# A two-layer MoE step on one core: the router moves into the output projection, its table is made on chip, the first expert and the extra tiles stay unsplit, and VectorE takes every low half of the experts' weights

## The reference, cut to what matters

```python
h = h + g1 * (merged @ w_out)                        # output projection, 1024x1024
u2 = rmsnorm(h, norm2_g) * (1.0 + sc2) + sh2         # sc2, sh2: one pair for latent, one for context
scores = softmax(u2 @ w_router)                      # 1024x16, 16 experts in 4 groups
# best group by its two best (scores + bias), then its two best experts; weights renormalised
y = sum over the token's 2 experts of  w * ((silu(u2 @ w_gate[e]) * (u2 @ w_up[e])) @ w_down[e])
h = h + g2 * y                                       # w_gate, w_up 1024x256; w_down 256x1024
```

## Time and profile before

| | |
|---|---|
| median of three runs | 2220.95 us |
| the profiled execution's own time | 2221.34 us |
| its span, first to last instruction | 2219.8 us (1.5 us lie around it) |
| busy share: TensorE, VectorE, ScalarE, POOL | 74%, 62%, 37%, 32% |
| mean granted clock of TensorE | 0.852 of 2.4 GHz |
| DMA: moved, mean rate | 303.96 MB, 137 GB/s |

### The profile page before, as it was taken

The page is one execution under the profiler, slowest core; times in us unless marked ns, Lnnn a source line. Parts: engine busy times, 40 slices in busy tenths (PEclk is TensorE's granted clock), DMA queues, the critical chain, the costliest instruction groups (busy, mean ns, idle before and its releaser), DMA issues.

```text
span 2219.8 us, 27630 instructions
## 1 busy us (share of the span) xinstructions
PE 1646.8 (74%) x8896; PEld 1399.6 (63%) x8896; DVE 1377.6 (62%) x2021; ACT 815.4 (37%) x1260; POOL 708.7 (32%) x303
## 2 busy tenths in 40 slices
PE   3799678778996941999338968777899886449970
PEld 1579455578996741777237955556899875437760
DVE  1457677889936362676362947778996356427744
ACT  3112555651123040666132225556212322126641
POOL 4222000024323133697133310000433232348951
PEclk6799789998998955999669978999999997569985
DMA  8221144312213431798621203441132162229956
GB/s 310 64 59 57 62 135 153 105 29 66 78 49 104 180 149 54 263 361 331 236 77 57 76 25 133 142 144 48 39 86 58 45 240 104 105 81 356 369 194 251
DMA packets 130409, 303.96 MB, mean 137 GB/s; under 512 B 11593, under 2 KB 81353, under 8 KB 109953
## 3 DMA queue, kind: packets, MB, share of 16 engines
q1 hardware_dynamic: 104096, 224.41, 29.5%
q10 hardware_dynamic: 10560, 40.90, 4.8%
q0 software_dynamic: 15600, 36.78, 4.7%
HBM read 279.76 MB, written 39.58 MB: 144 GB/s over the span
## 4 chain that ended last, share of the span: by engine, by line
PE 39%; DVE 21%; issue 18%; DMA 10%; POOL 6%; ACT 5%; DVEq 1%; ACTq 0%; POOLq 0%; SPq 0%
PE ps L484 10%; PE ps L470 5%; PE ps L662 5%; POOL w_lo L1941 4%; PE ps L548 4%; PE ps L720 3%; DMA raw<-in_w_down 3%; PE ps L416 2%; DVE probs L1455 2%; PE ps L528 2%; DVE gu_lo L1284 2%; PE ps L692 1%; PE ps L557 1%; PE ps L530 1%; DMA raw<-in_w_gate 1%
## 5 line engine op out<-in xcount | busy, mean ns | idle before, releaser
L1941 POOL TENSOR_TENSOR w_lo<-raw,w_hi 128x2048 fp32r<-128x2048 f32 (+1 forms) x68 | 299.8, 4414 | 738.6 <-ACT w_hi L944 704.6
L484 PE MATMUL ps<-u_hi,w_hi 128*128 128x320 f32 x768 | 245.2, 319 | 39.9 <-POOL w_lo L1941 30.1
L484 PE MATMUL ps<-u_lo,w_hi 128*128 128x320 f32 x768 | 243.4, 317 | 0.0
L484 PE MATMUL ps<-u_hi,w_lo 128*128 128x320 f32 x768 | 242.9, 316 | 0.0
L944 ACT ACTIVATE w_hi<-raw 128x2048 fp32r<-128x2048 f32 (+1 forms) x68 | 109.2, 1609 | 360.5 <-PE ps L470 155.4
L1566 DVE SCALAR_TENSOR_TENSOR cv<-glu,convw,cv 128x670 f32<-128x670 f32 x240 | 234.7, 1053 | 0.0
L484 PEld LDWEIGHTS ps<-u_hi,w_hi 128*128 128x128 f32 x768 | 149.6, 195 | 43.6 <-issue 33.3
L1471 DVE TENSOR_TENSOR pt_lo<-ps,pt_hi 128x512 fp32r<-128x512 f32 x160 | 108.6, 690 | 66.6 <-ACT pt_hi L1051 64.4
L484 PEld LDWEIGHTS ps<-u_hi,w_lo 128*128 128x128 f32 x768 | 149.6, 195 | 0.0
L484 PEld LDWEIGHTS ps<-u_lo,w_hi 128*128 128x128 f32 x768 | 149.5, 195 | 0.1
L720 PE MATMUL ps<-gu_hi,xt_hi 128*128 128x512 f32 x272 | 115.0, 423 | 37.6 <-DVE xt_lo L1770 27.1
(11 more groups left out here) (335 smaller groups left out, 4263.5 us busy)
## 6 DMA issues: line engine op xcount, KB each, us to landing
raw<-in_w_ada SPq DMA_DIRECT2D x52, 1024.0 KB, 8.8
raw<-in_w_in SPq DMA_DIRECT2D x48, 512.0 KB
raw_x<-in_w_gate SPq DMA_DIRECT2D x20, 1024.0 KB, 5.2
raw_x<-in_w_up SPq DMA_DIRECT2D x20, 1024.0 KB, 8.4
raw<-in_w_down SPq DMA_DIRECT2D x20, 1024.0 KB
raw<-in_w_gate SPq DMA_DIRECT2D x14, 1024.0 KB
raw<-in_w_up SPq DMA_DIRECT2D x14, 1024.0 KB
raw_x<-in_w_down SPq DMA_DIRECT2D x14, 1024.0 KB, 4.9
```

The lines of the kernel that those rows point to most:

```text
L484: ins = mm(ps[:, b, 0:HALF], (w_hi, w_lo)[w][:, s, cols(k):cols(k) + P], xs[x][:, k, half * HALF:(half + 1) * HALF], start=(k == 0 and w + ...
L1941: g_.tensor_tensor(w_lo[:, n % 2, 0:k], raw[:, n % 2, 0:k], w_hi[:, n % 2, 0:k].bitcast(F32), ALU.subtract).then_inc(*G.up("g_lo", "w_lo", n))
```

## The change

**Router.** The logits are taken from h_a before the norm: logits = rstd * (h_a @ (a2 * w_router)) + b2 @ w_router, with a2 = norm2_g * (1 + sc2) and b2 = sh2. a2 * w_router (`wr_a`) and b2 @ w_router (`blog`) are made during the conv projection; their columns are read by two DMAs on POOL (`c2col`) and one (`n2col`). In the last of the four units of the output projection TensorE transposes h_a tile by tile and takes the logits; product and sum of a tile stand together on VectorE, u2 follows tile by tile, and ScalarE takes Square and Sqrt per tile. Fifteen pair sums become three, 20 counting products become six (`cnt` has four empty tiles ahead of it).

**Table.** Each slot is split into a tile and a row; two one-hot arrays are written by VectorE, ten f32 products add up the table in PSUM, three VectorE steps take it out. Scatters, table in DRAM and its blanking are gone. `xe` is zeroed by ScalarE.

**First expert and extra tiles** use f32 weights as loaded (`gate_up_f`, `down_f`), without splits, in a place of their own that SyncE loads behind the output projection. The ring starts with expert 1; its two first low halves are written behind the table.

**Low halves.** Every low half of experts' weights is on VectorE, `w_down` too; POOL has gathers and scatters left. `ha_in` is read back ahead of the extra tiles, in another place.

```diff
# output projection, TensorE
             for nh in range(2):
-                bs = [fill(("wo", nh, t)) for t in range(NT)]
                 for kh in range(2):
                     for t in range(NT):
+                        if kh == 0:
+                            fill(("wo", nh, t), t)
+                        if nh + kh == 2:
+                            ha_transposes(t, 0)
...
+                        if nh + kh == 2 and t >= 1:
+                            ha_transposes(t - 1, 1)
+                        if nh + kh == 2 and t >= 2:
+                            logits(t - 2)
+            logits(NT - 2)
+            ha_transposes(NT - 1, 1)
+            logits(NT - 1)
...
+            for d in range(NT):
+                mm(ps[:, b, 0:NT * NE], (ones if d else tri)[:, :], flat(cnt[:, NT - 1 - d:2 * NT - 1 - d, :]), start=(d == 0), stop=(d == NT - 1))
+            mm(ps[:, b, 256:256 + NE], ones[:, :], csum5[:, :], start=True, stop=True).then_inc(*T.filled(("place",)))
+            eng.wait_ge(*T.at("at_tile"))
+            for x in range(2):
+                for t in range(NT):
+                    ins = mm(ps[:, b, 0:4 * MAXT], at_place[:, x, t, :], at_tile[:, x, t, :, :].rearrange("p f g -> p (f g)"),
+                             start=(x + t == 0), stop=(x == 1 and t == NT - 1))
# experts, TensorE
+            def gate_up_f():
+                for x in range(2):
+                    for k in range(KC):
+                        ins = mm(ps[:, 2, x * DE:(x + 1) * DE], xt_f[:, k, :], e0_gu[:, x, k, :], start=(k == 0), stop=(k == KC - 1))
+            def down_f():
+                for half in range(2):
+                    for c in range(2):
+                        ins = mm(ps[:, 4 + half, :], ht_f[:, c, :], e0_dn[:, c, half * 512:(half + 1) * 512], start=(c == 0), stop=(c == 1))
# SyncE
+            for e, k in GATE_UP_DOWN[0:4]:
+                unit(e, k)
+            eng.wait_ge(*S.at("filled", ("wo", 1, NT - 1)))
+            for k in range(2):
+                eng.dma_start(first_expert(k), io[part(k)][l, 0, :, :].rearrange("(p c) n -> p c n", p=P)).then_inc(*S.up(f"e0_raw{k}", "e0_in", k, by=16))
+            eng.wait_ge(*S.at("u2", NT - 1))
+            eng.dma_start(first_expert(2), io[part(2)][l, 0, :, :].rearrange("(p c) n -> p c n", p=P)).then_inc(*S.up("e0_raw2", "e0_in", 2, by=16))
...
-                eng.wait_ge(sems("ov_dn_lo"), o)
+                eng.wait_ge(sems("ov_gu"), o)
-                over(0, 2)
+                over(0)
+                over(1)
# ScalarE
+            for t in range(NT):
+                ha_tr(t, 0)
+                if t >= 1:
+                    spread(t - 1)
+                    ha_tr(t - 1, 1)
+            spread(NT - 1)
+            ha_tr(NT - 1, 1)
...
+            eng.wait_ge(*A.at("ha_out"))
+            act(xe[:, :, :], ident[:, 0:1].unsqueeze(2).broadcast_to([P, 2, D]), ACT.Copy, scale=0.0).then_inc(*A.up("a_xe", "xe_zero"))
             eng.wait_ge(*A.at("u2_out"))
             hi_expert(UNIT_OF[1, 0])
             hi_expert(UNIT_OF[1, 1])
# VectorE
+                    if nh and t >= 1:
+                        eng.wait_ge(*V.at("h_a", t - 1))
+                        u2_of(t - 1)
...
+            for x in range(2):
+                v.tensor_tensor(at_place[:, x, :, :], iot128[:, :].unsqueeze(1).broadcast_to([P, NT, P]),
+                                row_of[:, x, :].unsqueeze(2).broadcast_to([P, NT, P]), ALU.is_equal).then_inc(*V.step())
...
+            eng.wait_ge(*V.at("filled", ("table",)))
+            v.tensor_scalar(no_token[:, :], ps[:, b, 3 * MAXT:4 * MAXT], -float(SKIP), float(SKIP), ALU.mult, ALU.add).then_inc(*V.step())
+            v.tensor_copy(tab_w[:, :], ps[:, b, 2 * MAXT:3 * MAXT]).then_inc(*V.up("v_tab", "tab_w"))
+            v.tensor_tensor(tab_u[:, :, :], ps[:, b, 0:2 * MAXT].rearrange("p (f g) -> p f g", f=2),
+                            no_token[:, :].unsqueeze(1).broadcast_to([P, 2, MAXT]), ALU.add).then_inc(*V.drained(("table",)))
+            for k in range(2):
+                lo(UNIT_OF[1, k])
...
                 if e + 2 < NE:
                     lo(UNIT_OF[e + 2, 0])
                     lo(UNIT_OF[e + 2, 1])
+                if e + 1 < NE:
+                    lo(UNIT_OF[e + 1, 2])
# POOL
-            for n in range(U_MOE, U_MOE + 5):
-                lo(n)
+            eng.wait_ge(*G.at("drained", ("O", NH - 1)))
+            eng.wait_ge(*G.at("mod_out", 1))
+            for i in range(2):
+                dma(c2col[:, i, :, :].rearrange("p s (h c) -> p (s h) c", h=2),
+                    mod_d[i, SH2:SH2 + 2 * D].rearrange("(r p c) -> p r c", p=P, c=4), "c2_ld", "c2_in", i)
...
-                    eng.indirect_dma_start(out=tab_d, out_offset=bass.IndirectOffsetOnAxis(ap=slot_u[:, x, t:t + 1], axis=0),
...
-            g_.memset(xe[:, :, :], 0.0).then_inc(*G.up("g_c", "xe_zero"))
...
-                if e + 1 < NE:
-                    lo(UNIT_OF[e + 1, 2])
```

More of the change, by code:

```diff
@@ L62 @@
 U_MOE = U_OUT + N_OUT
[L63 to L64 removed]
+N_UNITS = U_MOE + 3 * (NE - 1)
+GATE_UP_DOWN = [(1, 0), (1, 1)]
 for e in range(NE - 1):
@@ L1577, in _ @@
                     conv_norm()
+            eng.wait_ge(*V.at("c2_in", 1))
+            eng.wait_ge(*V.at("small_loaded"))
+            for i in range(2):
+                v.scalar_tensor_tensor(out=c2col[:, i, 1, :], in0=c2col[:, i, 1, :], scalar=1.0, in1=n2col[:, :], op0=ALU.add, op1=ALU.mult).then_inc(*V.step())
+            eng.wait_ge(*V.at("v", V.steps))
+            for i in range(2):
+                v.tensor_tensor(wr_a[:, i, :, :], wr[:, :, :], c2col[:, i, 1, :].unsqueeze(2).broadcast_to([P, KC, NE]), ALU.mult).then_inc(*V.step())
+            ALIAS(("wr_a",), ("v", V.steps))
             for c in range(CCH):
@@ L1605, in _, with u2_of @@
                 k = V.steps
+            def u2_of(t):
+                eng.wait_ge(*V.at("std2", t))
+                v.reciprocal(rstd[:, t:t + 1], std[:, t:t + 1]).then_inc(*V.step())
+                eng.wait_ge(*V.at("v", V.steps))
+                v.scalar_tensor_tensor(out=u2[:, t, :], in0=h_a[:, t, :], scalar=rstd[:, t:t + 1], in1=a2_row[:, t // LT, :],
+                                       op0=ALU.mult, op1=ALU.mult).then_inc(*V.step())
+                eng.wait_ge(*V.at("v", V.steps))
+                v.tensor_tensor(u2[:, t, :], u2[:, t, :], b2_row[:, t // LT, :], ALU.add).then_inc(*V.up("v_u2", "u2", t))
             for nh in range(2):
@@ L1617, in _ @@
-            v.reciprocal(rstd[:, 0:NT], std[:, 0:NT]).then_inc(*V.step())
-            eng.wait_ge(*V.at("v", V.steps))
-            eng.wait_ge(*V.at("h_a", NT - 1))
-            for t in range(NT):
-                v.scalar_tensor_tensor(out=u2[:, t, :], in0=h_a[:, t, :], scalar=rstd[:, t:t + 1], in1=a2_row[:, t // LT, :],
-                                                     op0=ALU.mult, op1=ALU.mult).then_inc(*V.step())
-                eng.wait_ge(*V.at("v", V.steps))
-                v.tensor_tensor(u2[:, t, :], u2[:, t, :], b2_row[:, t // LT, :], ALU.add).then_inc(*V.up("v_u2", "u2", t))
@@ L1636, in _ @@
+            v.memset(cnt[:, 0:NT - 1, :], 0.0).then_inc(*V.step())
+            k_fixed = V.steps
+            eng.wait_ge(*V.at("h_a", NT - 1))
+            u2_of(NT - 1)
             eng.wait_ge(*V.at("filled", ("router",)))
             b = V.bank(("router",))
-            lgp = ps[:, b, 0:NT * NE].rearrange("p (t e) -> p t e", e=NE)
+            for t in range(NT):
+                ins = v.scalar_tensor_tensor(out=lg[:, t, :], in0=ps[:, b, t * NE:(t + 1) * NE], scalar=rstd[:, t:t + 1], in1=blog[:, t // LT, :],
+                                             op0=ALU.mult, op1=ALU.add)
+                ins.then_inc(*(V.drained(("router",)) if t == NT - 1 else V.step()))
@@ L1643, in _ @@
-            ALIAS(("lg_shift",), ("drained", ("router",)))
+            v.tensor_tensor(lg[:, :, :], lg[:, :, :], bc(ssq[:, 0:NT]), ALU.subtract).then_inc(*V.step())
+            ALIAS(("lg_shift",), ("v", V.steps))
             eng.wait_ge(*V.at("lg_exp"))
```

375 lines of the change are left out of this document (197 added, 178 removed).

## The result

The changed kernel takes 2126.81 us, the median of four runs (2123.27 to 2133.0), against 2219.02 for the kernel before in the same session: a ratio of 0.9589, 95% interval 0.956 to 0.9617, so 92 us less where 116 were forecast. The range for 8 in 10, 2082 to 2138, holds it; the forecast's own range, 2086 to 2123, does not. The profiled execution is the slowest of the four, 2133.0 us (span 2131.5); against the profiled execution of before, 2221.34, near the top of the kernel before's times (2215.3 to 2221.74), it gains 88.3.

What follows compares the result with a forecast made beforehand. Bound: the serial, idle path from output projection to first expert. Its terms bring the first silu 59 us earlier per layer, less 1 ahead of it: 2 x (59 - 1) = 116 off 2221.3, 2105 us; 8 in 10: 2082 to 2138.

Steps and rivals of the forecast that it cites:

- Router inside the output projection: Last quarter of the output projection: router work at 2.4 GHz takes 27.4 us, other engines hidden; gain 30 per layer.
- half-clock rival: Last quarter of the output projection: short instructions let the clock fall to 0.5; 27 us per layer, 2159; chance 6%.
- Small steps, counting: Softmax to mask, fewer steps and none on POOL, gain 11 us; mask to slots, fewer counting products, gain 6.
- Table: Slots to gather: table made on chip in 10.5 us, plus 1.9 for a gather beside a low half; gain 11.7.
- First expert: Gather's start to first silu: unsplit f32 products, 15.9 us against 16.2, landing 4.3; gain 0.
- The rival of u2's store: Ahead of the gather: stores and loads take twice 24 us, gather waits until 831; 14 per layer, 2133; chance 6%.
- Loop: Experts' loop: low halves moved from POOL to VectorE change nothing, 0; bounds 9 us less to 15 more per layer.
- the rival (20%): Experts' loop: VectorE becomes the bound, hx waiting behind w_down's low half; price 30 us, 2135; chance 20%.
- Extra tile: Extra tile: saved splits against slower f32 products and a gather meeting loads; 0, from 4 us less to 6 more.
- Ahead of it: Ahead of the output projection: added conv projection work costs 1 us more per layer (0 to 4); removed blanking 0.
- the rival at 10%: Router's ScalarE work: a table load for each Square and Sqrt; 4 us per layer, 2113; chance 10%.
- The signs named beforehand: Right: logits end 14 us behind last output matmul, VectorE near 98%; wrong: half clock, late hx, first silu after 850.

Runs made afterwards that it cites:

- three_buffers: Changed kernel with a third buffer for h_a's transposes and the last tile's second transposes ahead of the last but one tile's logits: 2108.14 us, ratio 0.951.
- loads_behind: Changed kernel with SyncE's restarting ring loads held until the first expert's tokens have landed: 2125.23 us, ratio 0.9575.
- lows_behind: three_buffers with expert 1's two first low halves on VectorE waiting until the first expert's tokens are transposed: 2106.6 us, ratio 0.9505.
- together_pool: three_buffers with wide_tick's store, h_a read back behind the extra tile, more of warm's products, and w_down's low half on POOL: 2087.52 us, ratio 0.9414.
- before_lows: Kernel before the change, with only the low half of w_down of experts 1 to 15 moved from POOL to VectorE: 2219.22 us, ratio 0.9993.
- warm: three_buffers with unused TensorE products added in the waits around the table and ahead of the extra tiles: 2104.97 us, ratio 0.9462.
- wide_tick: three_buffers with the small store at the start made 128 rows of 512 bytes instead of 4: 2104.41 us, ratio 0.9475.
- all: The last kernel: three_buffers with wide_tick, h_a read back behind the extra tile, added products as in warm, and lows_behind: 2078.65 us, ratio 0.9363.

## Why the prediction was right, and where its sizes were off

**Bound and direction: right.** The path from the last output product to the first expert was serial and idle, and what brought the first silu forward brought the loop forward: 50.4 and 50.2 us in the layers, with loops of about the same length. The mechanism of the forecast, given 55%, holds; its size does not: 24 of the 116 us are missing, and 2126.81 lies outside the 2086 to 2123 that the 55% stood for. That the wider range still holds it is luck in part: it was widened for VectorE, the store of u2 and the table loads, and none of these cost anything that the runs show. What cost the time, a loop of dependences and a small store, had nothing in the sum.

**Router inside the output projection: the term that failed.** "I cost them at 2.4 GHz" gave 27.4 us, "ends at 789.5"; the stretch took 36.8 (768.2 to 804.96). The step at fault is "Both are hidden; if that cover went, each us above 5.5 would cost up to five": I compared ScalarE's busy time per tile, under 3.5, with TensorE's 5.5, and did not follow its order. Its copy for tile t waits for the logits of t-2, because `ha_t` has two tiles, and TensorE's next transposes wait for that copy. It is a loop of dependences of 6.4 us per tile (TensorE's transposes start at 781.53 and 787.93) with no engine full. three_buffers shows it: 28.5. The half-clock rival (6%) was half right as to the place: two of five logits ran at 1.2 GHz, which cost 3.5 us; in three_buffers, without the idle time, about 1 of it is left.

**Small steps, counting: right**, 11.7 for 11 and 5.9 for 6; no VectorE step over 1 us is left from softmax to slots.

**Table: right.** 10.6 us from slots to gather where the sum said 10.5, well inside its bounds of 8 and 16. The gather in a low half's company cost 0.9 on the instruction (1.97 against 1.09), not 1.9. The sign was the one the row of before gave. The Trainium skill (SBUF — State Buffer, "Who interferes with whom") infers that a tensor_tensor leaves descriptor writing alone; the trace does not agree (1.97 against 1.09). The loads are not the cause: loads_behind holds them and the instruction still takes 1.97. lows_behind takes the low halves away and it falls to 1.09, and the gather that then lies beside one takes 2.44. In the whole trace of the changed kernel the 11 gathers beside no low half take 0.99 to 1.05 us, the 23 beside one 1.01 to 2.83. Whether such a gather waits in writing descriptors or in reading its row numbers, no run tells.

**First expert: 0 forecast, 1.3 lost** beyond the 1.9 that the sum had for the low half. "Landing 4.3" became 7.1, of which 0.9 are the low half's: I wrote that loads start again "as late behind it as before" and missed that the first two start with the gather (832.9 and 835.25). loads_behind puts 2.0 on them. The 16 products at 8.85 are what 6.9 and 1.7 gave, 8.6.

**Cover of the stores and loads: right.** The high half of expert 1 that waited for u2's store began at 819.0 and the gather at 831.9; with the gather 8 us earlier (three_buffers) it still started 1.7 us behind the last table product. The rival of u2's store falls.

**Loop: 0, right.** hx starts 1.6 to 2.0 us behind silu's end in 24 of 32 experts (silu 938.93, hx 941.26), each time right behind w_down's low half, as the rival said. With that low half on POOL the wait is gone, at most 0.5 us in all 32 (together_pool), and the time moves by nothing that can be told; before_lows shows the same from the other side. So VectorE's queue has the waits that the rival (20%) named, but not its price of 30 us. Why a loop takes 153 us once and 163 another time stays open.

**Extra tile: 0, right within its bounds**: from last silu to first combining step 0.7 gained in layer 1 (46.4 to 45.7) and 1.8 lost in layer 2 (44.0 to 45.7). Inside, in layer 1, the saved splits were given back to the gather, which lands in 7.9 us instead of 3.3, and to products partly at 1.2 GHz, 9.0 us (7.17 at the full clock in warm).

**Ahead of it: 2 forecast in all, 8.1 measured.** "The blanking that goes lay off the path: 0" named what went and not what came: a store of 4-byte rows. wide_tick shows it.

**Table loads:** one load ahead of the first Sqrt and none between the later Squares and Sqrts; the rival at 10% falls.

**The signs named beforehand** were mixed. Held: no VectorE step over 1 us. Missed: VectorE at 90% of 10.86 us, not near 98% of 10.5; logits that end 22.7 us behind where the last output matmul had ended, both counted from the projection's start, not 14; the ring's loads, of which two start 18 and 16 us ahead of the first silu and only the third 6 us behind it. Of the signs of being wrong, a first silu later than 850 came, at 850.98 (844.3 without the late start); the half clock came in two of five logits; and hx stood over 1 us behind silu in most experts, with DMA at 91% in layer 1's loop.

## What to carry to other kernels

When work is interleaved on two engines, follow one tile around the circle of buffers and queues before comparing busy times; a loop of dependences can be longer than either engine's work. When an instruction is replaced, price the replacement as well, tiny stores included. And where a serial path ends in idle waits, a few useless products that keep TensorE's clock up, or work and transfers held back until the one that is waited for has landed, shorten it further: each brought the first silu some 3 us forward per layer here (warm, lows_behind), of which the time of the whole kernel showed the first clearly and the second only with all the others (all).

## What the runs showed of the hardware

A store of 128 rows of 4 bytes took 33 us to land at the start and held a 1 MB load back by 5.5 us; 128 rows of 512 bytes took 27 and held up nothing (wide_tick). The Trainium skill (DMA: Bandwidth & Descriptors, "Specifications") says that transfers under 512 bytes are done as read-modify-write. The rows of 4 bytes agree with it in sign, but the kernel before wrote rows of 16 bytes there, and its load landed at 46.5 all the same; so where the limit lies no run here shows.

The granted clock fell to 0.58 while TensorE had no gap, in a stretch of short f32 products alone (three_buffers, 794.0 to 796.7), while the first expert, with products of 512 columns in the waits ahead of it, ran in the last kernel at a clock of 1.00 in 7.17 us, the same as in warm at 1019.0. So idle time alone does not explain the clock here.
